# Decoder step on one core: a third PSUM bank for attention transposes, decode softmax inside the prompt attention

## Chip, cores and metric

One core of one Trainium2 chip runs the whole program. The metric is the device time of one execution in microseconds (us), the median of several runs.

## What is computed

One inference step of a hybrid decoder layer for a prompt of 1024 tokens and eight sample tokens with one query each (d = 1024, float32):

```python
qa, ka, va, logf, ub, vb, qc, kc, vc, pd = project_in(x, w_in, b_forget)
o_a = fox(qa, ka, va, cumsum(logf))        # 4 heads x 64; samples: 2048 paged rows
o_b = gelu(ub) * spatial(layer_norm(gelu(vb)))
o_c = dilated(qc, kc, vc, bias)            # 4 heads x 64; windows (128,1) (512,4) (2048,16)
o_d = pool_out(pool_mix(pd))
x = LN(ALPHA * x + (gates(x) * branches).sum() @ w_out)
x = LN(ALPHA * x + moe(x))                 # 16 SwiGLU experts, 2 per token
# fox, prompt: logits = q k^T / 8 + f_q - f_k, causal, softmax, times v
```

## The kernel before

Every engine runs its own list of instructions, written out by hand; semaphores join them, and an engine that waits holds all that is behind it. The stages are: projections in tiles of 128 tokens (`project`, L1224); the forget bias (L1301, L1303); the prompt attention of branch A (`attention(0)`); the projections `qkc` and `vpd`, between which each `decode_slot` does a step of the samples' paged attention; the prompt attention of branch C (`attention(1)`); merge, router and experts (L460 to L462 and L595).

**Forget bias.** The bias is a running sum of log forget values, needed on all partitions for 1024 keys and 4 heads. Eight groups of 4 x 128 columns are made in banks 6 and 7 in turn: per tile one matmul with a triangle (sums inside the tile) and, for all tiles but the first, one with ones (sums before the tile). VectorE copies each group to `fb` (L1771).

**Attention.** A unit is a query tile (128 rows) and a pair of heads; a pair of units, tiles 2j and 2j+1, makes one item of `values`. There are 16 units, 0 to 15, with tiles 0, 1, 0, 1, 2, 3, 2, 3 and so on to 7; units 8 to 15 have more than four key blocks and are called wide here. In `attention(br)` TensorE does, per unit u: `scores(u + 1)` (L1321, with the causal mask L1329 in branch A; banks 0 to 3), for even u `values(u // 2 - 1)` (L1349 spreads the inverse sums in bank 7, L1358 multiplies by v in bank 6, semaphore `pv`), then `transposes(u, 0)` and `transposes(u, 1)` for the two heads (L1205). Up to four key blocks of weights are transposed into bank 4, the upper ones into bank 5. VectorE adds the bias and takes the extreme (`shifted`, L1801), ScalarE exponentiates (L1580, semaphore `ex`). ScalarE copies bank 4 to SBUF (`blocks`, L1590, semaphore `pt_free0`), VectorE copies bank 5 (L1811, `pt_free1`). As there is one bank of each kind, head 1's transposes wait until head 0's are copied:

```python
pe.wait_ge(S(f"pt_free{c}"), 32 * br + n if c == 0 else 16 * br + 2 * WIDE[u] + hh)
```

`norm(i)` on VectorE (L1828, L1829) multiplies values by inverse sums and raises `on`, which the next `values` wants. In branch C `values` also carries steps of the samples (`side`): products of window values in the upper halves of banks 7 and 6 (L1420), copied by `norm` (L1824), and at item 6 `heads_out` (L1428), copied by `decode_out` (L1778).

**Samples.** POOL gathers the paged keys and multiplies them by the queries (L1967), VectorE sums (`key_sums`, L1729). The softmax over pages (`decode_softmax`: L1878 to L1892) goes back and forth between VectorE, TensorE (`top`, `spread`, `total`) and ScalarE (L1610); it begins behind the first attention. SyncE issues the weight loads, and the bias table of branch C once the scores of branch A are read.

## Time and profile before

| | |
|---|---|
| median of three runs | 1555.1 us (1554.17 to 1555.33) |
| profiled execution | 1549.21 us, span 1547.4 |
| TensorE busy in the span | 1410.2 us, 91% |
| VectorE, ScalarE, GpSimd busy | 48%, 28%, 20% |
| mean granted TensorE clock | 0.955 |

The granted clock is that of TensorE as a share of full speed (2.4 GHz). A duration of an instruction reaches to its end; matmuls overlap, so their pace is the distance between starts. "Idle before" is the time in which an engine had nothing to do ahead of an instruction, with what ended it.

### The profile page before, as it was taken

How to read it: one execution, taken by the hardware profiler on the slowest of the kernel's cores; microseconds unless marked ns; L12 is line 12 of the kernel's file. 1: busy time of each engine (PE TensorE's matmuls, PEld its weight loads, DVE VectorE, ACT ScalarE, POOL GpSimd, SP SyncE). 2: the span in 40 equal slices, each digit the busy share in tenths (PEclk: the TensorE clock that was granted, in tenths of full speed). 3: DMA queues.
4: the chain of work that ended last, by engine and by line, in shares of the span. 5: the costliest groups of instructions: out<-in, count | busy, mean ns of one | idle time of the engine just before them, and what ended most of it. 6: DMA issues, size and time to landing. Idle time of an engine off the chain costs nothing.

```text
span 1547.4 us, 20002 instructions
## 1 busy us (share of the span) xinstructions
PE 1410.2 (91%) x7544; PEld 1064.3 (69%) x7544; DVE 743.7 (48%) x1302; ACT 435.6 (28%) x723; POOL 306.5 (20%) x233
## 2 busy tenths in 40 slices
PE   7989988799998899999999999999937999999980
PEld 3466465444454589999999999968835667766650
DVE  1276454322024552243343334464675667777746
ACT  1111124301106311111111111121223555566536
POOL 1138920045165000000000000000136112221220
PEclk9979999999989999999999999999957999999995
DMA  7346630155431113222231252232277999888645
GB/s 222 100 140 224 202 135 1 52 164 186 144 123 42 35 52 99 78 91 75 78 106 64 75 189 78 63 141 76 79 299 275 371 316 324 293 296 270 195 166 223
DMA packets 75197, 237.70 MB, mean 154 GB/s; under 512 B 17030, under 2 KB 27477, under 8 KB 61423
## 3 DMA queue, kind: packets, MB, share of 16 engines
q1 hardware_dynamic: 48630, 160.73, 28.7%
q0 software_dynamic: 17792, 59.20, 13.0%
q10 hardware_dynamic: 8704, 16.84, 3.2%
q8 instruction: 43, 0.70, 0.2%
q14 instruction: 28, 0.22, 0.0%
HBM read 213.49 MB, written 65.74 MB: 180 GB/s over the span
## 4 chain that ended last, share of the span: by engine, by line
PE 79%; DVE 6%; DMA 6%; ACT 4%; POOL 3%; issue 2%; SPq 0%; POOLq 0%; DVEq 0%; ACTq 0%
PE ps L460 15%; PE ps L462 15%; PE ps L461 15%; PE ps L1224 11%; PE ps L595 6%; PE ps L1205 5%; PE ps L1321 2%; PE ps L1358 2%; DMA b<-in_w 2%; POOL b L1967 2%; DMA b<-in_cache_k,b 2%; PE ps L1409 1%; PE ps L524 1%; ACT b L1590 1%; PE ps L1239 1%
## 5 line engine op out<-in xcount | busy, mean ns | idle before, releaser
L460 PE MATMUL ps<-b,b 128*128 128x344 f32 (+1 forms) x1360 | 469.1, 345 | 5.2 <-DVE b L816 2.7
L461 PE MATMUL ps<-b,b 128*128 128x344 f32 (+1 forms) x1360 | 465.1, 342 | 0.0
L462 PE MATMUL ps<-b,b 128*128 128x344 f32 (+1 forms) x1360 | 464.9, 342 | 0.0
L460 PEld LDWEIGHTS ps<-b,b 128*128 128x128 f32 x1360 | 254.9, 187 | 24.9 <-issue 4.2
L462 PEld LDWEIGHTS ps<-b,b 128*128 128x128 f32 x1360 | 254.9, 187 | 19.0
L461 PEld LDWEIGHTS ps<-b,b 128*128 128x128 f32 x1360 | 254.7, 187 | 16.8
L1224 PE MATMUL ps<-b,b 128*128 128x512 f32 (+1 forms) x640 | 257.9, 561 | 0.0
L1224 PEld LDWEIGHTS ps<-b,b 128*128 128x128 f32 x640 | 122.3, 194 | 121.5 <-issue 116.9
L991 DVE TENSOR_TENSOR b<-b,b 128x2048 fp32r<-128x2048 f32 x64 | 146.4, 2290 | 64.1 <-ACT b L681 63.9
L1205 PE MATMUL ps<-b,b 128*128 128x128 f32 (+1 forms) x782 | 122.2, 285 | 55.0 <-DMA b<-tmp_xs 21.9
L1205 PEld LDWEIGHTS ps<-b,b 128*128 128x128 f32 (+1 forms) x782 | 93.0, 146 | 105.0 <-issue 48.8
L1059 POOL DMA_INDIRECT tmp_xs<-b,b x36 | 42.3, 1175 | 600.0 <-issue 573.9
L624 ACT ACTIVATE b<-ps,b 128x344 f32<-128x344 f32 x96 | 52.6, 548 | 379.4 <-PE ps L462 379.4
L681 ACT CAST b<-b 128x2048 fp32r<-128x2048 f32 x64 | 122.2, 1913 | 27.2 <-DMA b<-in_w 23.6
L779 DVE TENSOR_TENSOR b<-b,ps 128x344 f32<-128x344 f32 x72 | 36.9, 513 | 181.8 <-PE ps L462 181.8
L595 PE MATMUL ps<-b,b 128*128 128x512 f32 x256 | 115.3, 593 | 0.5 <-ACT b L703 0.5
L1076 POOL DMA_INDIRECT tmp_yd<-b,b x32 | 66.3, 2073 | 248.9 <-DMA tmp_yd<-b,b 219.3
L1967 POOL TENSOR_TENSOR b<-b,b 128x2048 f32<-128x2048 f32 (+1 forms) x24 | 87.7, 3656 | 35.8 <-DMA b<-in_state_k 23.3
L595 PEld LDWEIGHTS ps<-b,b 128*128 128x128 f32 x256 | 46.2, 190 | 46.7 <-issue 45.9
L1801 DVE CUSTOM_DVE_ANT_0 b<-ps,b 128x128 f32<-128x128 f32 (+7 forms) x64 | 45.9, 755 | 49.0 <-PE ps L1329 24.8
L1580 ACT ACTIVATE b<-b,b 128x128 f32<-128x128 f32 (+7 forms) x64 | 49.8, 778 | 20.9 <-DVE b L1801 20.9
L1590 ACT COPY b<-ps 128x512 f32<-128x512 f32 (+3 forms) x64 | 32.1, 502 | 74.9 <-PE ps L1205 74.7
(265 smaller groups left out, 1257.0 us busy)
## 6 DMA issues: line engine op xcount, KB each, us to landing
b<-in_w SPq DMA_DIRECT2D x96, 1024.0 KB
b<-in_w_merge SPq DMA_DIRECT2D x32, 640.5 KB, 4.3
tmp_xs<-b ACTq DMA_DIRECT2D x32, 514.0 KB, 3.8
b<-tmp_xs SPq DMA_DIRECT2D x32, 514.0 KB
b<-in_w_in SPq DMA_DIRECT2D x8, 1024.0 KB, 8.6
b<-in_xT SPq DMA_DIRECT2D x4, 1024.0 KB, 12.4
b<-in_w_out SPq DMA_DIRECT2D x4, 1024.0 KB, 7.9
b<-in_x SPq DMA_DIRECT2D x8, 512.0 KB, 4.1
```

Source lines behind the costliest of these rows:

```text
L460: mm(out, hi, mhi, start=start, stop=False)
L461: mm(out, hi, mlo, start=False, stop=False)
L462: return mm(out, lo, mhi, start=False, stop=stop)
L595: m = mm(ps[:, 2 + c, :], hT[:, u, f, :], w2[q % 3][:, f, c * 512:(c + 1) * 512], start=(f == 0), stop=(f == 1))
L624: act.activation(sg[:, j % 2, :], ps[:, (j % 2) * 2, 0:CH], ACT.Sigmoid, bias=bias).then_inc(S("sgd"), 1)
L681: act.copy(w13_hi[m % 3][:].rearrange("p k n -> p (k n)"), w13_raw[m % 4][:].rearrange("p k n -> p (k n)")).then_inc(S("w13h"), 1)
L991: dve.tensor_tensor(lo, raw, hi.bitcast(F32), ALU.subtract).then_inc(S("w13l"), 1)
L1076: pool.indirect_dma_start(a["yd"], bass.IndirectOffsetOnAxis(rt["to"][:, q % 8:q % 8 + 1], 0), yo[:, u, :], None, bounds_check=TOK - 1, oo ...
L1205: return nc.tensor.transpose(out, in_, ident[0:n, 0:n])
L1224: m = mm(ps[:, j % 2, 0:cw], xT[:, k, t * P:(t + 1) * P], w_ring[:, n % 2, k, 0:cw], start=(k == 0), stop=(k == KD - 1))
L1580: act.activation(p_, p_, ACT.Exp, scale=-1.0, bias=am[:, n % 8:n % 8 + 1], accum_out=asum[:, n % 8:n % 8 + 1]).then_inc(S("ex"), 1)
L1967: pool.tensor_tensor(out, k, q, ALU.mult).then_inc(S("kq"), 1)
```

## The change

1. The forget bias: the 28 matmuls of sums before a tile become one of 32 columns in bank 3, copied to `dsum`; VectorE adds its columns while it copies a group.
2. Head 0's lower blocks are transposed into bank 4, head 1's into bank 7, upper blocks of both into bank 5. `values` keeps its inverse sums in the upper half of bank 6. ScalarE does both exponentials of unit u + 1 ahead of the copies of an even unit u, and it also takes the upper copies of odd units.
3. The softmax of the paged decode moves into `attention(0)`: matmuls in bank 5 in `values` of items 4, 5 and 7 (`STEPS_A`), VectorE's steps behind units 0, 5, 6, 7 and 14 and in `norm`, the exponential on ScalarE behind unit 13.
4. In branch C the samples' values go to bank 5, `heads_out` from item 6 to 7, `decode_out` behind the last `norm`. Where bank 5 holds such values, the upper transposes wait for `on`.

```diff
-        SLOTS_A = {i: ["top", "spread", "total"][i:i + 1] if i < 3 else [i - 3] for i in range(18)}
+        SLOTS_A = {i: [i - 3] if i >= 3 else [] for i in range(18)}
...
-        HEADS_C = 6
+        HEADS_C = 7
+        STEPS_A = {4: "top", 5: "spread", 7: "total"}
...
+                    pe.wait_ge(S("on"), 8)
...
                 for half in range(2):
                     if n >= 2:
                         pe.wait_ge(S("fb"), n - 1)
-                    elif n == 0:
-                        pe.wait_ge(S("ob"), 5)
                     for q in range(4):
-                        t = half * 4 + q
-                        o_ = ps[:, 6 + n % 2, q * P:(q + 1) * P]
-                        mm(o_, lf[:, t, h:h + 1].to_broadcast([P, P]), tri_neg[:], start=True, stop=(t == 0))
-                        if t:
-                            m = mm(o_, lpre[:, t, h:h + 1].to_broadcast([P, P]), ones_neg[:], start=False, stop=True)
+                        m = mm(ps[:, 6 + n % 2, q * P:(q + 1) * P], lf[:, half * 4 + q, h:h + 1].to_broadcast([P, P]), tri_neg[:],
+                               start=True, stop=True)
                     m.then_inc(S("fb_mm"), 1)
                     n += 1
+                    if n == 2:
+                        mm(ps[:, 3, 0:32], ones_neg[:], lpre[:].rearrange("p t h -> p (t h)"), start=True, stop=True).then_inc(S("fb_mm"), 1)
...
-                        pe.wait_ge(S(f"pt_free{c}"), 32 * br + n if c == 0 else 16 * br + 2 * WIDE[u] + hh)
+                        if c == 1:
+                            pe.wait_ge(S("pt_free1"), 16 * br + 2 * WIDE[u] + hh)
+                            if hh == 0 and u // 2 - 1 in ((STEPS_A, VALUES_C)[br]):
+                                pe.wait_ge(S("on"), 8 * br + u // 2)
+                        elif n:
+                            pe.wait_ge(S("pt_free0"), 32 * br + n - 1)
+                        bank = 5 if c else (4, 7)[hh]
                         for k in range(4 * c, min(qt + 1, 4 * c + 4)):
-                            m = tr(ps[:, 4 + c, (k % 4) * P:(k % 4 + 1) * P], pbuf[br][n % 4][:, k * P:(k + 1) * P])
+                            m = tr(ps[:, bank, (k % 4) * P:(k % 4 + 1) * P], pbuf[br][n % 4][:, k * P:(k + 1) * P])
...
-                            mm(ps[64 * hh:64 * hh + 64, 7, a_ * P:(a_ + 1) * P], arec[:, col:col + 1].to_broadcast([P, 64]), ident[:],
+                            mm(ps[64 * hh:64 * hh + 64, 6, W + a_ * P:W + (a_ + 1) * P], arec[:, col:col + 1].to_broadcast([P, 64]), ident[:],
...
+                pe.wait_ge(S("ltot"), 1)
+                mm(ps[:, 5, 0:32], trisA[:], ltot[:], start=True, stop=True).then_inc(S("lsuf"), 1)
...
+            def side_a(i):
+                step = STEPS_A.get(i)
+                if step == "top":
+                    pe.wait_ge(S("pt_free1"), 2 * WIDE[2 * i + 2])
+                    pe.wait_ge(S("dmx"), 1)
+                    tr(ps[:, 5, 0:P], mx[:]).then_inc(S("dmx_tr"), 1)
+                elif step == "spread":
+                    pe.wait_ge(S("pt_free1"), 2 * WIDE[2 * i + 2])
+                    pe.wait_ge(S("dmc"), 1)
+                    mm(ps[:, 5, 0:32], mcol[0:32, 0:1].to_broadcast([32, P]), ident[0:32, 0:32],
+                       start=True, stop=True).then_inc(S("dmb"), 1)
+                elif step == "total":
+                    pe.wait_ge(S("pt_free1"), 2 * WIDE[2 * i + 2])
+                    pe.wait_ge(S("dsum"), 1)
+                    mm(ps[:, 5, 0:32], ones[:], dsum[:], start=True, stop=True).then_inc(S("dtot"), 1)
+
+            attention(0, bias_a, lambda k, h: va[:, k, h * 64:h * 64 + 64], side_a, tail_a)
...
-                    m = mm(ps[32 * r:32 * r + 32, bank, W:2 * W], pC[:, w:w + 32], values_c(b)[:, r, :], start=True, stop=True)
+                    m = mm(ps[32 * r:32 * r + 32, 5, half * W:(half + 1) * W], pC[:, w:w + 32], values_c(b)[:, r, :], start=True, stop=True)
...
-                for n, b in enumerate(VALUES_C.get(i, ())):
-                    values_of_c(b, 7 - n)
+                if i in VALUES_C:
+                    pe.wait_ge(S("pt_free1"), 16 + 2 * WIDE[2 * i + 2])
+                for half, b in enumerate(VALUES_C.get(i, ())):
+                    values_of_c(b, half)
                 if i == HEADS_C:
-                    heads_out(1, 7)
+                    pe.wait_ge(S("pt_free1"), 32)
+                    heads_out(1, 5)
...
-                             ps[:, 4, 0:nb * P].rearrange("p (k r) -> p k r", r=P)).then_inc(S("pt_free0"), 1)
+                             ps[:, (4, 7)[hh], 0:nb * P].rearrange("p (k r) -> p k r", r=P)).then_inc(S("pt_free0"), 1)
+
+                def high_blocks(u, hh):
+                    qt, hp = UNITS[u]
+                    if qt >= 4:
+                        act.wait_ge(S("pt1"), 16 * br + 2 * WIDE[u] + hh + 1)
+                        act.copy(pT_of(br, hh)[:, 4:qt + 1, P:2 * P],
+                                 ps[:, 5, 0:(qt - 3) * P].rearrange("p (k r) -> p k r", r=P)).then_inc(S("pt_free1"), 1)
 
                 weights(0, 0)
                 weights(0, 1)
-                for u in range(16):
+                for u in range(0, 16, 2):
+                    weights(u + 1, 0)
+                    weights(u + 1, 1)
+                    blocks(u, 0)
+                    blocks(u, 1)
                     for hh in range(2):
-                        blocks(u, hh)
-                        if u < 15:
-                            weights(u + 1, hh)
+                        blocks(u + 1, hh)
+                        high_blocks(u + 1, hh)
+                    if br == 0 and u == 12:
+                        act.wait_ge(S("dsh"), 1)
+                        act.activation(sA[:], sA[:], ACT.Exp).then_inc(S("dex"), 1)
+                    if u < 14:
+                        weights(u + 2, 0)
+                        weights(u + 2, 1)
...
+            dve.wait_ge(S("fb_mm"), 3)
+            link(dve.tensor_copy(dsum[:], ps[:, 3, 0:32]))
             for n in range(8):
-                dve.wait_ge(S("fb_mm"), n + 1)
-                dve.tensor_copy(fb[:, n // 2, (n % 2) * 512:(n % 2) * 512 + 512], ps[:, 6 + n % 2, :]).then_inc(S("fb"), 1)
+                if n >= 2:
+                    dve.wait_ge(S("fb_mm"), n + 2)
+                first = dsum[:].rearrange("p (t h) -> p h t", h=H)[:, n // 2, 4 * (n % 2):4 * (n % 2) + 4]
+                dve.tensor_tensor(fb[:, n // 2, (n % 2) * 512:(n % 2) * 512 + 512].rearrange("p (t r) -> p t r", r=P),
+                                  ps[:, 6 + n % 2, :].rearrange("p (t r) -> p t r", r=P),
+                                  first.rearrange("p (t o) -> p t o", o=1).to_broadcast([P, 4, P]), ALU.add).then_inc(S("fb"), 1)
...
-                        if u % 2 == 0:
-                            dve.wait_ge(S("pv"), 8 * br + u // 2)
-                        dve.tensor_copy(pT_of(br, hh)[:, 4:qt + 1, u % 2 * P:u % 2 * P + P],
+                        dve.wait_ge(S("pv"), 8 * br + u // 2)
+                        dve.tensor_copy(pT_of(br, hh)[:, 4:qt + 1, 0:P],
...
-                    if br:
-                        for n, b in enumerate(VALUES_C.get(i, ())):
-                            dve.tensor_copy(vo[:, b, :], ps[:, 7 - n, W:2 * W]).then_inc(S("vo"), 1)
-                        if i == HEADS_C:
-                            decode_out(1, 7)
+                    if br == 0:
+                        softmax_step(STEPS_A.get(i))
+                    else:
+                        for half, b in enumerate(VALUES_C.get(i, ())):
+                            dve.tensor_copy(vo[:, b, :], ps[:, 5, half * W:(half + 1) * W]).then_inc(S("vo"), 1)
                     to = oT[:, 2 * br, hp, j * 2 * P:(j + 1) * 2 * P]
-                    link(dve.tensor_copy(to, ps[:, 7, 0:2 * P]))
-                    dve.tensor_tensor(to, ps[:, 6, 0:2 * P], to, ALU.mult).then_inc(S("on"), 1)
+                    link(dve.tensor_copy(to, ps[:, 6, W:2 * W]))
+                    dve.tensor_tensor(to, ps[:, 6, 0:W], to, ALU.mult).then_inc(S("on"), 1)
...
-                    blocks(u, 0)
-                    blocks(u, 1)
+                    if u % 2 == 0:
+                        blocks(u, 0)
+                        blocks(u, 1)
...
+            def softmax_step(step):
+                if step == "top":
+                    dve.wait_ge(S("dmx_tr"), 1)
+                    dve.tensor_reduce(mcol[0:32, :], ps[0:32, 5, 0:P], AX.X, ALU.max).then_inc(S("dmc"), 1)
+                elif step == "spread":
+                    dve.wait_ge(S("dmb"), 1)
+                    link(dve.tensor_copy(mrow[:], ps[:, 5, 0:32]))
+                    dve.tensor_tensor(sA[:], sA[:], mA, ALU.subtract).then_inc(S("dsh"), 1)
+                elif step == "total":
+                    dve.wait_ge(S("dtot"), 1)
+                    link(dve.reciprocal(drec[:], ps[:, 5, 0:32]))
+                    dve.tensor_tensor(sA[:], sA[:], rA, ALU.mult).then_inc(S("dp"), 1)
+
+            def side_a(u):
+                if u == 0:
+                    dve.wait_ge(S("lsuf"), 1)
+                    link(dve.tensor_copy(drec[:], ps[:, 5, 0:32]))
+                elif u == 5:
+                    dve.wait_ge(S("lgb"), 16)
+                    link(dve.tensor_tensor(ltot[:], drec[:], lgb[:], ALU.add))
+                    link(dve.tensor_tensor(lfs[:, 0], lfs[:, 0],
+                                           ltot[:].rearrange("p (b o h) -> p b o h", b=NB, o=1).to_broadcast([P, NB, 16, H]), ALU.add))
+                elif u == 1:
                     key_sums(15)
+                elif u == 6:
+                    dve.wait_ge(S("ks"), 16)
+                    link(dve.scalar_tensor_tensor(s16, s16, SCALE, lfs[:, 0], ALU.mult, ALU.add))
+                elif u == 7:
+                    dve.wait_ge(S("selfd0"), N("selfd0", 16))
+                    link(dve.tensor_scalar(sA[:, :, 16, :], sA[:, :, 16, :], SCALE, None, ALU.mult))
+                    dve.tensor_reduce(mx[:, 0:32].rearrange("p (b h) -> p b h", b=NB), sA[:].rearrange("p b r h -> p b h r"),
+                                      AX.X, ALU.max).then_inc(S("dmx"), 1)
+                elif u == 14:
+                    dve.wait_ge(S("dex"), 1)
+                    dve.tensor_reduce(dsum[:].rearrange("p (b h) -> p b h", b=NB), sA[:].rearrange("p b r h -> p b h r"),
+                                      AX.X, ALU.add).then_inc(S("dsum"), 1)
...
-            last_norm = attention(1, lambda h, qt: tb[:, h, SEQ - P - P * qt:SEQ], lambda u: None)
+            last_item = attention(1, lambda h, qt: tb[:, h, SEQ - P - P * qt:SEQ], lambda u: None)
+            def last_norm():
+                last_item()
+                decode_out(1, 5)
+
```

TensorE at the start of the forget bias (`lf`, `lpre` are the sources of the sums, `fb` the semaphore of copied groups), before:

```order
L1301 MATMUL ps<-b_97984_108,b_210544_74 128x128 [waits ob,lpre,lf]
L1301 MATMUL ps<-b_97984_108,b_210544_74 128x128
L1303 MATMUL ps<-b_98496_109,b_210688_75 128x128
L1301 MATMUL ps<-b_97984_108,b_210544_74 128x128
L1303 MATMUL ps<-b_98496_109,b_210688_75 128x128
L1301 MATMUL ps<-b_97984_108,b_210544_74 128x128
```

and now, from the first group to the first scores:

```order
L1300 MATMUL ps<-b_97984_108,b_210544_74 128x128 [waits ob,lpre,lf]
L1300 MATMUL ps<-b_97984_108,b_210544_74 128x128 x7
L1305 MATMUL ps<-b_210688_75,b_98496_109 128x32
L1300 MATMUL ps<-b_97984_108,b_210544_74 128x128 [waits fb]
...
L1300 MATMUL ps<-b_97984_108,b_210544_74 128x128 [waits fb]
L1300 MATMUL ps<-b_97984_108,b_210544_74 128x128 x3
L1385 MATMUL ps<-b_96832_105,b_96960_106 128x32 [waits qkT_qka,ltot,evicted,fb]
L1321 MATMUL ps<-b_148480_55,b_140288_54 128x128 x2
```

Of the pairs of L1301 and L1303 only the triangles are left (L1300), with one matmul for all sums (L1305); L1385, for the decode's sums, stood behind the attention.

ScalarE around units 10 and 11 of `attention(0)`, before (`b_132096` and `b_164864` take the transposed weights of head 0 and 1):

```order
L1590 COPY b_132096_119<-ps 128x4x128 [waits pv,pt0]
L1580 ACTIVATE b_49536_115,b_211104_82<-b_49536_115,b_211072_81 128x768 [waits sc_free]
L1590 COPY b_164864_120<-ps 128x4x128 [waits pv,pt0]
L1580 ACTIVATE b_53632_116,b_211104_82<-b_53632_116,b_211072_81 128x768 [waits sc_free]
L1590 COPY b_132096_119<-ps 128x4x128 [waits pt0]
L1580 ACTIVATE b_201232_113,b_211104_82<-b_201232_113,b_211072_81 128x896 [waits sc_free]
L1590 COPY b_164864_120<-ps 128x4x128 [waits pt0]
L1580 ACTIVATE b_205328_114,b_211104_82<-b_205328_114,b_211072_81 128x896 [waits sc_free]
```

and now:

```order
L1603 ACTIVATE b_49536_115,b_211104_82<-b_49536_115,b_211072_81 128x768 [waits sc_free]
L1603 ACTIVATE b_53632_116,b_211104_82<-b_53632_116,b_211072_81 128x768 [waits sc_free]
L1613 COPY b_132096_119<-ps 128x4x128 [waits pv,pt0]
L1613 COPY b_164864_120<-ps 128x4x128 [waits pv,pt0]
L1613 COPY b_132096_119<-ps 128x4x128 [waits pt0]
L1620 COPY b_132096_119<-ps 128x2x128 [waits pt1]
L1613 COPY b_164864_120<-ps 128x4x128 [waits pt0]
L1620 COPY b_164864_120<-ps 128x2x128 [waits pt1]
L1603 ACTIVATE b_201232_113,b_211104_82<-b_201232_113,b_211072_81 128x896 [waits sc_free]
L1603 ACTIVATE b_205328_114,b_211104_82<-b_205328_114,b_211072_81 128x896 [waits sc_free]
```

Both exponentials of unit 11 have moved ahead of the copies of unit 10; the two copies of `128x2x128` are the upper blocks of unit 11, from VectorE.

VectorE at unit 12 of `attention(0)` (`b_92672` holds the paged scores), before:

```order
L1828 COPY b_33024_50<-ps 128x256 [waits pv]
L1829 TENSOR_TENSOR b_33024_50<-ps,b_33024_50 128x256 [waits dve_chain]
L1811 COPY b_132096_119<-ps 128x3x128 [waits pv,pt1]
L1811 COPY b_164864_120<-ps 128x3x128 [waits pv,pt1]
L1801 ISA b_201232_113,b_211072_81<-ps,b_173056_58 128x896 [waits pt1,sc]
```

and now:

```order
L1843 ISA b_53632_116,b_211072_81<-ps,b_173056_58 128x1024 [waits pt1,sc]
L1843 ISA b_211072_81 128x1
L1902 COPY b_96448_102<-ps 128x32 [waits dmb,pv]
L1903 TENSOR_TENSOR b_92672_91<-b_92672_91,b_96448_102 128x544 [waits dve_chain]
L1869 COPY b_33024_50<-ps 128x256
L1870 TENSOR_TENSOR b_33024_50<-ps,b_33024_50 128x256 [waits dve_chain]
L1852 COPY b_132096_119<-ps 128x3x128 [waits pv,pt1]
L1852 COPY b_164864_120<-ps 128x3x128 [waits pv,pt1]
```

The copy and subtraction L1902 and L1903 stand between the shifts and `norm`, thus ahead of `on`.

## Rows read from the trace of the kernel before

**Rows 1.** Stretch A:B, length; busy PE, PEld, DVE, ACT, POOL (x instructions); clock; DMA; GB/s

```profile
192.40:211.90 19.50, 15.55 (x125) 15.16 (x122) 10.70 (x13) 0.82 (x1) 10.87 (x5) 0.91 0.77 274
...
199.20:203.40 4.20, 4.20 (x23) 4.20 (x24) 1.18 (x2) 0.00 (x0) 3.09 (x3) 0.59 0.68 260
...
211.90:302.10 90.20, 78.89 (x608) 50.10 (x608) 39.33 (x103) 41.50 (x101) 0.00 (x0) 1.00 0.03 10
302.10:309.23 7.13, 1.42 (x6) 0.98 (x6) 5.12 (x12) 0.00 (x0) 3.23 (x6) 0.75 0.53 149
466.10:549.83 83.73, 71.52 (x560) 43.27 (x561) 42.38 (x116) 40.00 (x96) 19.48 (x23) 0.98 0.11 36
```

**Rows 2.** TensorE in order of time, forget bias (L1301, L1303): start, duration, idle before

```profile
199.15 0.71 PE L1301 MATMUL ps<-b,b 128*128 128x128 f32 x4 [3.17 <-DVE b L1771]
...
206.24 0.39 PE L1301 MATMUL ps<-b,b 128*128 128x128 f32 x2
```

**Rows 3.** Waits in the two attentions: us in total, times, longest

```profile
DVE b L1801 <- PE ps L1329: 24.8, 15, 2.5
...
PE ps L1205 <- ACT b L1590: 9.7, 17, 0.8
...
PE ps L1205 <- ACT b L1590: 8.9, 16, 0.8
```

**Rows 4.** TensorE in order of time: transposes of units 5 and 13

```profile
229.92 0.60 PE L1205 MATMUL ps<-b,b 128*128 128x128 f32 x4
231.29 0.63 PE L1205 MATMUL ps<-b,b 128*128 128x128 f32 x4 [0.77 <-ACT b L1590]
...
273.89 1.04 PE L1205 MATMUL ps<-b,b 128*128 128x128 f32 x8
275.25 0.63 PE L1205 MATMUL ps<-b,b 128*128 128x128 f32 x4 [0.33 <-ACT b L1590]
...
277.22 1.99 PE L1321 MATMUL ps<-b,b 64*128 64x512 f32 x8
```

**Rows 5.** Groups of instructions (busy, mean ns of one | idle before), and one piece of VectorE's time

```profile
L1729 DVE TENSOR_REDUCE b<-b 128x32 f32<-128x2048 f32 x16 | 36.4, 2284 | 21.3 <-POOL b L1967 20.8
...
L1829 DVE TENSOR_TENSOR b<-ps,b 128x256 f32<-128x256 f32 x16 | 6.8, 424 | 0.6
...
L1801 DVE CUSTOM_DVE_ANT_0 b<-ps,b 128x896 f32<-128x896 f32 x8 | 8.4, 1088 | 5.9 <-PE ps L1329 3.4 <-PE ps L1321 2.5
...
L1590 ACT COPY b<-ps 128x512 f32<-128x512 f32 x40 | 23.2, 581 | 56.1 <-PE ps L1205 56.1
...
L1771 DVE COPY b<-ps 128x512 f32<-128x512 f32 x8 | 5.4, 688 | 8.0 <-PE ps L1303 8.0
...
L1801 DVE CUSTOM_DVE_ANT_0 b<-ps,b 128x128 f32<-128x128 f32 (+7 forms) x64 | 45.9, 755 | 49.0 <-PE ps L1329 24.8
L1580 ACT ACTIVATE b<-b,b 128x128 f32<-128x128 f32 (+7 forms) x64 | 49.8, 778 | 20.9 <-DVE b L1801 20.9
...
507.63 0.76 DVE L1824 COPY b<-ps 128x256 f32<-128x256 f32 x2 [2.29 <-PE ps L1358]
```

**Rows 6.** TensorE, then VectorE, in order of time behind the first attention

```profile
307.82 0.48 PE L1205 MATMUL ps<-b,b 128*128 128x128 f32 x1 [4.29 <-DVE b L1878]
...
309.23 8.73 PE L1224 MATMUL ps<-b,b 128*128 128x512 f32 x16
...
318.38 7.11 PE L1224 MATMUL ps<-b,b 128*128 128x512 f32 x16
...
306.66 1.10 DVE L1878 TENSOR_REDUCE b<-b 128x32 f32<-128x544 f32 x1
...
309.56 0.72 DVE L1884 TENSOR_TENSOR b<-b,b 128x544 f32<-128x544 f32 x1
```

**Rows 7.** End of the second attention: VectorE's `decode_out`, TensorE's weight loads of the merge

```profile
539.54 0.70 DVE L1778 COPY b<-ps 64x8 f32<-64x8 f32 x4 [6.93 <-PE ps L1358]
...
554.37 0.19 PEld L460 LDWEIGHTS ps<-b,b 128*128 128x128 f32 x1 [0.78 <-DVE b L794]
```

31 lines of the change are left out of this document (7 added, 24 removed).

## The prediction

> **What bounds the kernel now.** I read first the busy time by stretch [rows 1]. TensorE is busy for 78.9 of the 90.2 us of the first attention and 71.5 of the 83.7 us of the second, VectorE and ScalarE for about half or less: TensorE's own order sets the pace, and only its gaps can be won. Around the first attention stand two worse stretches: before it 19.5 us with TensorE busy for 15.6, and behind it 7.1 us (302.1 to 309.2) with 1.4 busy. Then come the waits [rows 3]: in each attention the transposes wait 16 or 17 times for the copy L1590 of ScalarE, 9.7 and 8.9 us together. The last step is the order of time on TensorE at the places which the change touches [rows 2, 4, 6].
>
> **1. Forget bias.** Now there are 32 + 28 matmuls. At full clock a record follows the one before by 0.11 us (two in 0.39, of which the last one's own length is 0.28), and each matmul has two records: 0.22 [rows 2]. Two groups of four are made, then TensorE waits 3.17 us until VectorE (late with sums of keys) starts to copy, and six groups follow from 199.15. The granted clock over 199.2 to 203.4 is 0.59 [rows 1], so mostly the lower of the two levels (1.2 GHz), behind that gap. In the change one matmul replaces 28, and the addition goes into the copy (L1771, 0.69 a group). I leave its price as it is, because `norm`'s product L1829 reads 256 columns of a bank and a buffer in 0.42 where the plain copies L1824 take 0.38 each [rows 5]; 0.04 more a group stays under TensorE's 0.9. A copy of 32 columns is put ahead, so the six groups start at 199.4. With the clock low until 203.4 as now, about ten of their 24 matmuls are done by then, and 14 x 0.22 = 3.1 remain: 206.4, the last addition 207.2, the small matmul for the decode sums, first scores at 207.5 where they start at 211.9 now. **-4.4 us.** Bounds: the gap is now 4.9 us long, and a low clock for another 2 us costs 1 (-3.4); no low clock at all gives -5.8.
>
> **2. Transposes, narrow units** (query tiles 0 to 3; units 0 to 7). The transposes of head 1 start 1.37 us behind those of head 0 for four blocks (229.92, 231.29) [rows 4]; a block takes 0.11 (eight in 1.04, less the last one's length), so 0.93 is lost. In total, the waits and 0.17 for each modelled end: 9.7 + 17 x 0.17 = 12.6, and 8.9 + 16 x 0.17 = 11.6. With head 1 in bank 7 its transposes follow at once. The eight narrow units lose 0.6 to 0.9 each, some 6.3 together. Not all comes back. In unit 0 and 1 ScalarE now does both exponentials of unit 1 ahead of the first copies, and the sum of keys on VectorE (2.3 us) holds the reciprocal: 0.7 stays. Behind unit 7 the scores of the next tile need both banks of each head, thus both of VectorE's shifts of the unit before (1.09 each for tile 6 [rows 5], so some 0.8 for tile 4), while the transposes of unit 7 now take only 0.9: 0.7 late. **-4.9, and -5.0 in the second attention.**
>
> **3. Wide units** (tiles 4 to 7; units 8 to 15). Bank 5 is still single, so head 1's upper blocks wait for head 0's upper copy. An odd unit with tile 7 takes 3.33 us now (273.89 to 277.22) [rows 4]. Then: lower blocks to 0.44, upper to 0.88; ScalarE's lower copy from 0.64 to 1.12 and its upper one to 1.6 (0.58 busy [rows 5], 0.1 of it overlapped); head 1's upper blocks 1.66 to 2.1. That saves 1.2; tile 5 by the same sum 0.7 to 1.3. In an even unit VectorE's norm must be over first (two of 0.42), then its upper copy: 1.5 to 1.9 us instead of 2.1 to 3.0. The even units 10 and 12 of each attention get a new wait: their upper blocks wait for `on`, as bank 5 holds decode values. Queued behind it are head 1's transposes and the next scores. In the first attention `norm` does a small maximum more in unit 10 (gain nil) and in unit 12 a copy and the subtraction of 0.72 [rows 6]: `on` 2.0 us behind `pv`, the unit 1.1 us slower than now. In the second it does two copies (0.76) first, 0.5 us slower each. Further, the scores of units 11 to 13 wait about 0.4 once for VectorE's shifts, which were hidden behind longer transposes. Unit by unit, 8 to 15: 0.6 + 0.7 + 0 + 0.8 - 1.1 + 1.2 + 1.1 + 0.3 = **-3.6**; in the second attention 0.6 + 0.8 - 0.5 + 0.8 - 0.6 + 1.4 + 2.0 (units 14 and 15 together) = **-4.5**.
> Bounds on 2 and 3 together: nothing if each wait comes back elsewhere, 28 if none does (24 and the few waits for L1811). Around my 18 I keep 5 to 24.
>
> **4. Softmax of the paged decode.** Behind the first attention TensorE stands while VectorE norms, adds and takes a maximum (4.29 idle before 307.82) [rows 6], and goes on at 309.23: the first projection of 16 records takes 8.73 us, the one at 318.38 takes 7.11. The change puts these steps into the units: adds and maximum on VectorE at units 5 to 7, the exponential on ScalarE behind unit 13, the sum at unit 14. What hides them: VectorE idles 24.8 us in 15 pieces before its shifts [rows 3], and the longest new step (maximum 1.10) at unit 7 ends just before `values` wants the reciprocal; ScalarE's exponential lies behind 6 us of scores and values. If that cover is gone, the steps' length comes back, about 4 us. Gone: 7.1 of the gap and 1.6 of the slow projection, **-8.7**. Added in the attention: three small matmuls of about 0.3, **+0.9**. `on` = 8 is now wanted by the transposes behind the next projection, 7 us later, so it is hidden. The gathers on POOL and SP's weights are issued behind the same semaphores as now and keep their distances.
>
> **5. End of the second attention.** The 32 tiny matmuls move from `values(6)` to `values(7)` at the same cost, and `decode_out` goes behind the last norm: 0.84 us (0.70 and its link) [rows 7] ahead of VectorE's split, for which TensorE waits 0.78 already. All of it is late: **+0.8**.
>
> **Sum:** -4.4 - 4.9 - 3.6 - 5.0 - 4.5 - 8.7 + 0.9 + 0.8 = **-29.4 us**. The profiled execution takes 1549.2 (span 1547.4) and would take 1519.8; the median of the three runs, 1555.1, is 5.9 above it, and 1555.1 - 29.4 gives **1526 us**. What comes after (merge, experts) starts earlier and is as before. About 0.2%, 3 us, is what a measurement can tell from no change.
>
> **Rivals.**
> A, *the attention becomes a chain of latencies* (22%). Without waits for bank 4 TensorE runs into exponentials and shifts that are some tenths late in every unit. For it: two such places came up above, both in narrow units. Against it: both helpers are half idle. Then the attentions give 5 in place of 18: 1526 + 13 = 1539.
> B, *ScalarE's new order* (3%), the slow side. The copies of an even unit now stand behind both exponentials of the next unit. If the scores of that unit end only as the transposes start, each copy comes one shift (mean 0.76) and two exponentials (mean 0.78) [rows 5] later, 2.3 us; over 16 even units 37: 1526 + 37 = 1563. It decides where the scores end less than 2.3 us ahead of the transposes. `values` lies between, above 3 us in the last pairs but about 1 in the first, whose exponentials are short; so it can bite only there.
> C, *the clock* (1%). The granted clock is 1.00 over the first attention and 0.98 over the second, with 33 gaps of up to 0.8 us in them [rows 1, 3]: such gaps do not lower it here. Should three banks in turn lower it for a quarter of the 150 us of busy time, 37 are lost as well: 1563. The Trainium skill, "TensorE: Matmul & The Clock Gate", section "A second HAM failure mode: psum-queue depth-cycling", tells of a kernel in which cycling through banks left small idles that made the clock swing, and so speaks against this change; by that rule the time would be C's. No run here shows it for gaps of this size.
> D, *the softmax in the units does not hide* (8%): 4 us on VectorE, and 3 more at `on`: 1526 + 7 = 1533.
> My forecast has the remaining 66%.
>
> **Range.** Low: -5.8 in 1, -24 in 2 and 3 and the rest as forecast give -37, or 1518; all at once is unlikely, and I take 1519. High: 1539, A. B and C, 4%, lie outside, with the lower half of A's outcomes. Faster by over 0.2%: 0.94; within 0.2%: 0.02; slower: 0.04.
>
> **What would show it.** First scores 4 to 5 us earlier; the transposes' waits for copies under 5 us in an attention instead of 9; the first attention at about 83 us, the second at 74; no gap behind the first attention, and the first projection there at 7.1 us; a wait of 1 to 1.5 us before the upper transposes of units 10 and 12; TensorE's wait for the split at 1.6 instead of 0.8. The prediction is wrong if as many waits for exponentials replace those for copies, if scores wait for shifts in all wide units, or if the clock falls inside an attention.

## The result and the profile after

The changed kernel takes 1535.83 us (median of 4 runs, 1534.79 to 1536.08) against 1554.63 for the kernel before on the same chip (1552.33 to 1555.33). The ratio is 0.9887, with a 95% interval of 0.9872 to 0.9902. The medians lie 18.8 us apart (1.1% by the ratio): faster as forecast and inside the range, but less than two thirds of the 29.4 us. The profiled execution takes 1534.79 (span 1533.0, granted clock 0.952), 14.4 us less span than before: the profiled execution of before (1549.21) was 5.4 us below its median, that of after 1.0 below, so the stages below account for 14.4 us and not for all of the gain.

The windows of after that answer to [rows 1] (length; busy PE, PEld, DVE, ACT, POOL, each with its count of instructions; clock; DMA; GB/s), the last two being new:

```profile
191.00:199.40 8.40, 2.11 (x20) 2.00 (x18) 5.33 (x6) 0.77 (x1) 5.79 (x3) 0.93 0.89 289
199.40:203.40 4.00, 3.14 (x14) 3.14 (x15) 2.06 (x4) 0.00 (x0) 2.12 (x1) 0.50 0.54 213
...
209.40:294.30 84.90, 79.03 (x614) 50.94 (x613) 40.13 (x105) 45.69 (x110) 0.08 (x1) 1.00 0.09 33
294.30:301.30 7.00, 7.00 (x19) 3.11 (x18) 2.98 (x8) 0.00 (x0) 3.23 (x6) 1.00 0.38 121
...
354.00:370.70 16.70, 13.08 (x100) 6.23 (x99) 2.30 (x4) 1.37 (x5) 8.83 (x12) 0.80 0.57 191
...
520.90:533.00 12.10, 12.01 (x66) 9.09 (x64) 0.00 (x0) 0.09 (x1) 0.00 (x0) 0.58 0.01 1
```

The first attention is 84.9 us instead of 90.2 and TensorE never stands behind it. Two stretches are new trouble: TensorE is busy for 13.1 of 16.7 us from 354.0, and its clock is 0.58 over the last 12 us of the second attention.

Waits of TensorE in the first attention, then in the second (total, times, longest), to be set beside [rows 3]:

```profile
PE ps L1206 <- DVE b L1870: 2.0, 2, 1.4
PE ps L1206 <- ACT b L1620: 1.1, 4, 0.3
...
PE ps L1321 <- DVE b L1843: 0.8, 2, 0.7
...
PE ps L1206 <- DVE b L1852: 0.6, 3, 0.2
PE ps L1206 <- ACT b L1613: 0.4, 1, 0.4
...
PE ps L1206 <- DVE b L1870: 2.3, 2, 1.1
PE ps L1206 <- ACT b L1620: 1.1, 4, 0.3
```

The 9.7 and 8.9 us for ScalarE's copies have become 0.4 + 1.1 and 0.5 + 1.1; the largest wait that is left is the new one for `on` (L1870). The length of a projection behind the attention answers to [rows 6]: 7.13 where it was 8.73.

Now the two places where time was lost. TensorE in order of time (start, duration, idle before): the forget bias, `values_a(6)` with the projection behind it, and the heads of the second attention.

```profile
191.02 1.95 PE L1300 MATMUL ps<-b,b 128*128 128x128 f32 x16
192.81 0.31 PE L1305 MATMUL ps<-b,b 128*128 128x32 f32 x2
200.26 8.04 PE L1300 MATMUL ps<-b,b 128*128 128x128 f32 x48 [7.15 <-DVE b L1811]
...
360.00 1.93 PE L1433 MATMUL ps<-b,b 128*32 128x256 f32 x16 [3.62 <-issue]
361.87 8.91 PE L1225 MATMUL ps<-b,b 128*128 128x512 f32 x16
...
521.04 5.70 PE L1452 MATMUL ps<-b,b 128*128 128x2 f32 x32
```

Then the products of keys on GpSimd and VectorE's sum and additions at the forget bias, and GpSimd's gathers of values, in order of time:

```profile
192.55 4.51 POOL L2037 TENSOR_TENSOR b<-b,b 128x2048 f32<-128x2048 f32 x1
197.10 2.29 DVE L1765 TENSOR_REDUCE b<-b 128x32 f32<-128x2048 f32 x1 [2.81 <-POOL b L2037]
...
199.52 1.29 DVE L1811 TENSOR_TENSOR b<-ps,b 128x512 f32<-128x512 f32 x2
...
201.28 4.62 POOL L2037 TENSOR_TENSOR b<-b,b 128x2048 f32<-128x2048 f32 x1 [4.22 <-DMA b<-in_cache_k,b]
...
316.52 1.03 POOL L2001 DMA_INDIRECT b<-in_cache_v,b  x1 [0.17 <-issue]
317.55 1.64 POOL L2020 DMA_DIRECT2D b<-in_state_k  x3
...
323.72 1.80 POOL L2037 TENSOR_TENSOR b<-b,b 128x768 f32<-128x768 f32 x1 [4.00 <-DMA b<-in_state_k]
325.69 1.00 POOL L2001 DMA_INDIRECT b<-in_cache_v,b  x1 [0.16 <-issue]
...
353.85 1.03 POOL L2001 DMA_INDIRECT b<-in_cache_v,b  x1 [0.16 <-issue]
```

The additions start behind VectorE's sum of keys 14 (197.10), and that behind the product of keys 14 (192.55 to 197.07). The product with a wait of 4.22 us (201.28) is that of keys 15; it ends at 205.9, long behind the first addition, and its sum is made in the attention (213.81).

A wait "for issue" on TensorE names no releaser, but `values_a(6)` waits for nothing late other than the sixth gather, `load_values(6)`. That gather is issued at 353.85 and TensorE wants it at 356.4 (360.00 - 3.62). A step of GpSimd's chain (gather, window keys, 4 us of waiting for them, product) takes 9.2 us here (325.69 - 316.52); TensorE's slot takes 8.5 to 8.9 and is the faster of the two. In the kernel before, the same gather was issued 10 us ahead of its use:

```profile
362.94 1.03 POOL L1931 DMA_INDIRECT b<-in_cache_v,b  x1 [0.16 <-issue]
...
372.94 1.05 PE L1409 MATMUL ps<-b,b 128*32 128x256 f32 x16
```

Because many experiments follow, I cut each trace at the same places of TensorE's order. The lengths in us: A, first forget-bias matmul to first scores; B, from there to the first 128x512 projection matmul behind the attention's last scores; C, to `values_a(0)`; D, to the last `values_a`; E, to the first scores of the second attention; F, to the first matmul of the merge. "Start" is the moment of the first cut. It differs by up to 6.5 us between executions although no edit lies ahead of it, the part behind the last cut by up to 3.5 us (997.6 to 1001.1), and E and F by some us with the clock. The runs were taken in rounds on different chips, each with the kernel before beside it (medians 1552.8 to 1554.6), so "won" is counted from the before of the same round; between rounds this is the fairer number.

| kernel | start | A | B | C | D | E | F | median us | won |
|---|---|---|---|---|---|---|---|---|---|
| before | 192.5 | 19.4 | 79.2 | 34.8 | 113.8 | 26.4 | 83.7 | 1554.6 | - |
| after | 191.0 | 18.4 | 73.5 | 26.2 | 120.3 | 24.6 | 79.0 | 1535.8 | 18.8 |
| e1_bias_alone | 190.9 | 17.4 | 79.2 | 35.6 | 113.9 | 27.2 | 83.8 | 1553.4 | 1.1 |
| e2_softmax_back | 192.6 | 15.5 | 69.9 | 36.2 | 117.8 | 26.4 | 77.3 | 1536.0 | 18.6 |
| e3_values_first | 192.5 | 15.4 | 73.5 | 26.2 | 113.9 | 28.7 | 77.3 | 1527.9 | 26.7 |
| e4_sums_behind | 193.9 | 12.9 | 74.3 | 26.2 | 119.6 | 30.4 | 79.0 | 1534.5 | 20.0 |
| e5_old_order | 189.6 | 18.9 | 76.4 | 26.2 | 120.5 | 27.5 | 79.5 | 1535.3 | 18.5 |
| e6_one_bank | 192.6 | 17.7 | 80.1 | 26.2 | 121.3 | 27.5 | 89.6 | 1547.3 | 6.4 |
| e9_before_values_first | 191.9 | 19.9 | 79.2 | 34.6 | 113.9 | 27.5 | 88.1 | 1553.3 | 0.4 |
| e10_back_values_first | 192.4 | 15.6 | 69.9 | 36.5 | 113.9 | 27.4 | 77.3 | 1533.8 | 19.9 |
| e8_both | 192.9 | 11.3 | 74.3 | 26.2 | 113.8 | 26.6 | 77.3 | 1525.1 | 27.7 |
| e11_reader | 194.2 | 16.2 | 72.5 | 26.2 | 113.8 | 26.4 | 74.4 | 1525.2 | 27.6 |
| e12_all_three | 189.7 | 12.1 | 73.3 | 26.2 | 113.8 | 27.0 | 76.0 | 1519.4 | 33.4 |
| e13_bias_undone | 187.7 | 15.5 | 73.3 | 26.2 | 113.9 | 26.1 | 74.4 | 1523.6 | 29.7 |

### The profile page after: what moved, and what is told of

Its sections match the earlier page's. It is cut to its first block, busy times and chain, and to the rows that moved or that the text cites. A ratio compares the mean times of both kernels' runs of the same rounds, so it can differ in the third digit from the quotient of the medians.

```text
span 1533.0 us, 19911 instructions
## 1 busy us (share of the span) xinstructions
PE 1404.3 (92%) x7490; PEld 1059.1 (69%) x7490; DVE 730.0 (48%) x1288; ACT 442.2 (29%) x739; POOL 302.7 (20%) x233
## 4 chain that ended last, share of the span: by engine, by line
PE 79%; DMA 6%; DVE 5%; POOL 4%; ACT 3%; issue 2%; SPq 0%; POOLq 0%; DVEq 0%; ACTq 0%
PE ps L461 15%; PE ps L463 15%; PE ps L462 15%; PE ps L1225 11%; PE ps L596 6%; PE ps L1206 5%; POOL b L2037 3%; PE ps L1364 2%; PE ps L1321 2%; DMA b<-in_w 2%; DMA b<-in_cache_k,b 1%; PE ps L1433 1%; PE ps L525 1%; PE ps L1240 1%; DMA tmp_yd<-b,b 1%
## 5 line engine op out<-in xcount | busy, mean ns | idle before, releaser
L463 PEld LDWEIGHTS ps<-b,b 128*128 128x128 f32 x1360 | 254.9, 187 | 19.4 <-issue 0.8
L1206 PE MATMUL ps<-b,b 128*128 128x128 f32 (+1 forms) x782 | 118.8, 285 | 37.2 <-DMA b<-tmp_xs 21.5
L682 ACT CAST b<-b 128x2048 fp32r<-128x2048 f32 x64 | 122.3, 1913 | 26.4 <-DMA b<-in_w 22.7
L1077 POOL DMA_INDIRECT tmp_yd<-b,b x32 | 63.2, 1974 | 252.7 <-DMA tmp_yd<-b,b 223.2
L2037 POOL TENSOR_TENSOR b<-b,b 128x2048 f32<-128x2048 f32 (+1 forms) x24 | 87.5, 3648 | 40.8 <-DMA b<-in_state_k 23.3
L1765 DVE TENSOR_REDUCE b<-b 128x32 f32<-128x2048 f32 x16 | 36.5, 2284 | 34.3 <-POOL b L2037 34.1
```

What stands on the lines that cost most here:

```text
L463: return mm(out, lo, mhi, start=False, stop=stop)
L682: act.copy(w13_hi[m % 3][:].rearrange("p k n -> p (k n)"), w13_raw[m % 4][:].rearrange("p k n -> p (k n)")).then_inc(S("w13h"), 1)
L1077: pool.indirect_dma_start(a["yd"], bass.IndirectOffsetOnAxis(rt["to"][:, q % 8:q % 8 + 1], 0), yo[:, u, :], None, bounds_check=TOK - 1, oo ...
L1206: return nc.tensor.transpose(out, in_, ident[0:n, 0:n])
L2037: pool.tensor_tensor(out, k, q, ALU.mult).then_inc(S("kq"), 1)
```

## The experiments

**e1, the forget-bias edit alone on the kernel before** (part 1 of the change, nothing else).

> The kernel before with the forget-bias edit alone (one matmul for the sums of whole tiles, added by VectorE in its copy). In the full change the stage became 1.0 us shorter where 4.4 were forecast: TensorE stood 7.15 us instead of 3.17 before the first addition, because VectorE's sum of keys waited for GpSimd's product, and that 4.22 us for a gather of keys. Theory M (a matter of the moment at which the gather runs): the edit does not touch the gathers, so with the wait at about 3.2 us the first scores start 3.4 to 4.4 us earlier than in before, and the time is 3 to 4.5 us shorter. Rival S (structural: the shorter work of TensorE always meets VectorE's late sums of keys): the wait is near 5 to 7 us and only 0.5 to 1.5 us are won. In both the attentions are as in before.

Measured: 1553.42 us, ratio 0.999 (0.9974 to 1.0007), so no gain that can be told from none. A is 2.0 us shorter. TensorE waited 5.96 us for the first addition: it came to this stage 1.5 us earlier than in before (190.9 instead of 192.5) and was through its two groups sooner, but the additions could start only at the same time (TensorE goes on at 198.98, in before at 199.15). That is rival S, whose numbers fit as well (5 to 7 us of wait, 0.5 to 1.5 us won). The gather of keys on which the expectation puts the 7.15 us belongs to keys 15, and nothing at the forget bias waits for those.

**e2, the softmax back behind the attention** on the changed kernel.

```diff
-        STEPS_A = {4: "top", 5: "spread", 7: "total"}
+        STEPS_A = {}
-            qk_evict("qkc", 1, 1)
+            decode_softmax(0, sA, lambda: qk_evict("qkc", 1, 1), lambda: None)
```

> The full change with only the paged softmax put back behind the first attention (adds, maximum, exponential, sum, product and the three small matmuls as before). Theory G (given back): in the changed kernel the gap behind the attention went (8.8 us), but the stage of the next projections became 6.3 us longer, because GpSimd's chain of window keys and value gathers, 9.1 to 9.6 us a step against TensorE's 8.5 to 8.9, had its slack in that gap; so putting the softmax back costs only about 2.5 us (between 1 and 4), the gap of about 8.8 us returns and the wait of 3.6 us before values_a(6) is gone. Rival N (the 6.3 us have another cause, for example the new order of the gathers or a disturbed run): putting it back costs 8 us or more and the stage keeps its 130 us.

Measured: 1535.98, ratio 0.9868 (0.9837 to 0.99), nothing lost on the median. C shows the gap back, 36.2 for 26.2:

```profile
295.06 0.47 PE L1206 MATMUL ps<-b,b 128*128 128x128 f32 x1 [4.64 <-DVE b L1939]
```

B is 3.6 us shorter without the softmax in the units. So the move takes 10.0 out and puts 3.6 in, and the rest of its worth went elsewhere. D is 117.8 and not 113.8, as GpSimd once waited 7.14 us for window keys and `values_a(8)` then 2.08 for its gather: even with the gap the slack can be used up.

**e3, each gather of values one step earlier** on GpSimd, nothing else changed.

```diff
+            pool.wait_ge(S("dv"), 1)
+            load_values(2)
             key_step_c(0)
             key_step_c(1)
-            for s in range(2, 16):
-                pool.wait_ge(S("dv"), s - 1)
-                load_values(s)
-                if s < NB:
-                    pool.wait_ge(S("ks"), 16 + s - 1)
-                    keys_c(s)
-                    key_step_c(s)
+            for s in range(3, 17):
+                if s <= NB:
+                    pool.wait_ge(S("ks"), 16 + s - 2)
+                    keys_c(s - 1)
+                if s < 16:
+                    pool.wait_ge(S("dv"), s - 1)
+                    load_values(s)
+                if s <= NB:
+                    key_step_c(s - 1)
```

> The full change with one edit on GpSimd: each gather of values is issued one step earlier, ahead of the product of window keys of the step before (load_values(2) before key_step_c(0), load_values(s) before key_step_c(s-1)). Theory G: the wait of 3.6 us before values_a(6) at 360 us and the low clock behind it (0.9 + 1.8 us) come from the gather of values that was issued too late; with the edit both go, and the kernel takes 5.5 to 6.5 us less than the changed one (near 1529.5). Rival N (the wait is for something else, or the window keys then come late for VectorE): less than 2 us won, the wait stays or turns up before the transposes.

Measured: 1527.9, ratio 0.9823 (0.9795 to 0.9851), 7.9 us less than the changed kernel; D fell by 6.5. GpSimd in order of time now waits for TensorE, not the other way round, and TensorE goes from the tiny matmuls straight into `values_a(6)`:

```profile
343.85 1.03 POOL L2001 DMA_INDIRECT b<-in_cache_v,b  x1 [3.02 <-PE ps L1433]
```

```profile
352.97 1.94 PE L1222 MATMUL ps<-b,b 128*8 128x128 f32 x64
354.72 1.05 PE L1433 MATMUL ps<-b,b 128*32 128x256 f32 x16
355.70 4.56 PE L1225 MATMUL ps<-b,b 128*128 128x512 f32 x10
```

**e4, the sum of keys 14 behind the additions** of the forget bias.

```diff
-                key_sums(6 + i)
+                if i < 8:
+                    key_sums(6 + i)
...
+            key_sums(14)
+            dve.wait_ge(S("ks"), 15)
```

> The full change with VectorE's sum of keys 14 moved from ahead of the forget-bias additions to behind them. Theory: the 7.15 us wait before the first addition shrinks to about 2 (additions start once the queries of the last tile are out, 194.3), the clock behind it stays higher, the sum costs up to 1.3 us before the first shift: 3 to 5 us less than the changed kernel. Rival (the stage is bound by GpSimd's chain anyhow, since sums 14 and 15 are only moved): under 1 us won, with a wait of 2 us or more in the first units of the attention.

Measured: 1534.54, ratio 0.986 (0.983 to 0.989). A is 5.5 us shorter (wait 2.18 instead of 7.15), B 0.8 longer, E 5.8 longer: there TensorE waited 3.17 us (after: 1.50) for a copy that VectorE makes behind the write of `out_pool`, a transfer, and the clock was low for 13.7 us of E instead of 3.4. On the median only 1.3 us is left, which the scatter (1528.5 to 1539.2) covers. Inconclusive by itself.

**e5, ScalarE's old order in even units.**

```diff
-                    weights(u + 1, 0)
-                    weights(u + 1, 1)
                     blocks(u, 0)
+                    weights(u + 1, 0)
                     blocks(u, 1)
+                    weights(u + 1, 1)
```

> The full change with one edit: in even units ScalarE copies a head's lower blocks before it takes the next unit's exponential of that head, as before the change (copy, exponential, copy, exponential, where the change has two exponentials, then two copies). Theory (the order is worth little once each head has a bank of its own): both attentions stay within 1 us of the changed kernel, first scores to last scores 60.5 and 55.7 us, and the time within 2 us. Rival B (the new order delays each copy by a shift and two exponentials): this kernel is then 5 us or more faster than the changed one. Rival B' (the new order is what makes three banks work): this kernel is 4 us or more slower.

Measured: 1535.26, ratio 0.9884 (0.9859 to 0.9909), the same as the changed kernel. B is 2.9 longer in a profiled execution that was the slowest of four (clock 0.97 over the first 62.5 us, where after has 1.00), and first to last scores of the second attention 57.0 instead of 55.7. Of the 2.9 us, 1.7 are the low clock (3.4 us of it at half speed), so the new order is worth about 1 us an attention in the traces; the medians do not show it (1535.3 against 1535.8). Rival B, by which this kernel had to be 5 us faster, is out, and so is B'.

**e6, also the lower transposes of both heads in bank 4 again.**

```diff
-                        elif n:
-                            pe.wait_ge(S("pt_free0"), 32 * br + n - 1)
-                        bank = 5 if c else (4, 7)[hh]
+                        else:
+                            pe.wait_ge(S("pt_free0"), 32 * br + n)
+                        bank = 5 if c else 4
```

> The full change with the old order of ScalarE as in the run before and, in addition, the lower transposes of both heads in bank 4 again (each group waits for the copy of the one before). Theory (parts 2 and 3: the second bank takes the waits for copies away): first scores to last scores grow from 60.5 to about 65.5 us in the first attention and from 55.7 to about 61.5 in the second, and the kernel takes 8 to 12 us more than the run with old order and two banks. Rival A (the attention is a chain of latencies, banks hardly matter): under 4 us more, with the waits for exponentials and shifts smaller by what the waits for copies grow.

Measured: 1547.3, ratio 0.996 (0.9946 to 0.9975), 12.0 us more than e5. The waits for copies are back (these are those of the first attention; the second has 8.6 as well):

```profile
PE ps L1206 <- ACT b L1613: 8.6, 15, 0.8
```

The other waits of that attention shrank from 4.3 us in e5 to 0.9, so some of what A describes is there, but rival A's "under 4 us" is out. (F of 89.6 overstates it: the clock was 0.67 over the first 20.6 us of that attention.)

**e9, the early gathers on the kernel before.** The edit of e3.

> The kernel before with the edit on GpSimd alone (each gather of values issued one step earlier). The runs so far: with this edit the changed kernel came to 1527.9 us from 1535.8, and the changed kernel with the softmax put back took 1536.0, with a wait of 2.1 us before a values_a too. Theory G (only the changed kernel lacks slack): no more than 1 us won on 1554.6, and the stage from values_a(0) to the last values_a stays at 113.8 us. Rival V (in before too, some executions wait for the gathers, which is why the median of its runs lies above the profiled one): 2 to 5 us won on the median, and less scatter between its runs.

Measured: 1553.29, ratio 0.9995 (0.9982 to 1.0009): no gain, D 113.9. Theory G holds and rival V falls.

**e10, softmax back and early gathers.** The edits of e2 and e3.

> The full change with the softmax put back behind the attention and the gathers of values issued one step earlier. With the late gathers the move of the softmax was worth nothing (1536.0 with it put back, 1535.8 in the changed kernel). By the traces the move takes 10.0 us out between the first projection and values_a(0) (36.2 to 26.2) and puts 3.6 us into the first attention (69.9 to 73.5 from first scores to the first projection). Theory G (the late gathers hid the gain): here the gap is back and nothing waits for gathers, so this kernel takes 5 to 7 us more than the 1527.9 of the changed kernel with the early gathers, near 1534. Rival (the move gains nothing whatever the gathers do): 1526 to 1530.

Measured: 1533.81, ratio 0.987 (0.9844 to 0.9896). With late gathers the move of the softmax was worth 0.2 us (1536.0 against 1535.8), with early ones 5.9 (1533.8 against 1527.9; 6.8 by what each won over the before of its round), where the traces promise 10.3 - 3.6 = 6.7. A wait of TensorE ahead of a `values_a`, of 2.1 to 4.5 us, stands in the profiled executions of all five kernels that have the changed attention and late gathers (after, e2, e4, e5, e6), and in none of the seven with early ones.

**e8, early gathers and the sum behind the additions.** The edits of e3 and e4.

> The changed kernel with the early gathers of values and, in addition, the sum of keys 14 behind the forget-bias additions (each alone: 1527.9 and 1534.5). By the traces the moved sum makes the stretch from the first forget-bias matmul to the first scores 12.9 us instead of 15.4, while the first attention takes 0.8 us more and the bands 1.8. Theory (additive, the price of the bands is a matter of one execution): 1 to 3 us less than 1527.9. Rival (what is won ahead of the attention is lost behind it, where VectorE waits for a transfer): within 1 us of 1527.9.

Measured: 1525.06, ratio 0.982 (0.9803 to 0.9837), 2.8 us less than e3. Over the before of its own round it won 27.7 and e3 26.7, so the medians do not tell the theory (1 to 3 us) from the rival (within 1). The traces speak for the theory: A and B together take 85.6 us where e3 has 88.9, and E is 26.6, so the long E of e4 was a matter of that execution.

**e11, early gathers, and the upper transposes freed by the last read of bank 5.**

```diff
-                                pe.wait_ge(S("on"), 8 * br + u // 2)
+                                if br:
+                                    pe.wait_ge(S("vo"), N("vo", NB + 1 + VALUES_C[u // 2 - 1][1]))
+                                else:
+                                    pe.wait_ge(S("five"), {4: 1, 5: 2, 7: 3}[u // 2 - 1])
```

> The changed kernel with the early gathers of values, and the upper transposes of the units that share bank 5 with decode values wait for the last read of that bank (a semaphore behind the maximum, the copy or the reciprocal, or that of the two decode copies) instead of for the norm's product behind it. Theory (the waits of 2.0 and 2.3 us in the attentions are the norm's two operations, 0.8 us each time, and the rest is the reads themselves): the waits shrink to about 0.8 and 0.9 us, and 1.5 to 3 us are won, near 1525.5. Rival (VectorE's upper copy stands behind the norm anyway and the wait only moves to head 1's transposes): under 1 us won, the wait for L1852's copies grows by as much.

Measured: 1525.17, ratio 0.9829 (0.9815 to 0.9842), 2.7 us less than e3 on the median, but 0.9 by what each won in its round. In the traces B is 1.0 shorter and F 2.9, of which 1.3 lie ahead of the last scores and 1.6 behind them, where the clock was low for 3.4 us instead of 6.8. Waits of the first attention, then of the second:

```profile
PE ps L1206 <- DVE b L1855: 1.8, 4, 1.0
```

```profile
PE ps L1206 <- DVE b L1870: 0.7, 2, 0.4
```

In the first attention 1.2 us of the wait moved to the upper copy (0.6 before), as the rival said; in the second it really went (2.3 to 0.7).

**e12, all three edits.**

> The changed kernel with all three edits: early gathers, sum 14 behind the additions, upper transposes released by the last read of bank 5. If the three are additive, by the traces: 2.5 - 0.8 us from the sum and 1.5 to 3 us from the release, 1523 to 1526. If the release only moves a wait, 1526 to 1528.

Measured: 1519.37 (1516.25 to 1522.45), ratio 0.9784 (0.9766 to 0.9802). It is below what was expected and the fastest of all: 33 us under the kernel before, 16 under the changed one. It is 5.7 us under e8 and 5.8 under e11, of the same round, where the traces show 2.3 (B and first to last scores) and 3.3 (A and B) for the edit that was added. In the profiled executions 3.2 of the 4.3 us that e12 has less than e8 lie ahead of the first cut, where the code is the same. So the excess over the sum is not explained by the edits.

**e13, the forget bias as before** in the kernel of e12: 60 matmuls, plain copies.

> The fastest kernel so far (all three edits, 1519.4) with the forget bias as before: 60 matmuls in eight groups, plain copies. There VectorE's sum of keys no longer stands ahead of the copies, so this prices the forget-bias edit without that delay. Theory (the matmuls left out are on the path as soon as VectorE is not late): 21 of the 27 matmuls left out belong to the six groups behind the first copies, at 0.22 us each at full clock 4.6 us, so first forget-bias matmul to first scores grows from 12.1 to 16.5 to 17.5, and the time by 4 to 5.5 us, to about 1524. Rival (the edit is worth 1 us or so whatever VectorE does, as its worth of 1.0 in the changed kernel and 1.1 alone suggest): under 2 us more.

Measured: 1523.6, ratio 0.9809 (0.9795 to 0.9823), 4.2 us more on the median (3.8 by what each won in its round), though the two intervals overlap a little. A grows from 12.1 to 15.5, 3.4 us. The edit is worth its matmuls once VectorE is not late.

## Why the prediction was right, and where it was too high

**Forget bias: -4.4 forecast, -1.0 in A, 2.5 us earlier first scores.** The count of matmuls and the price of an addition (0.69) were right. The step that failed was the wait, taken as "now 4.9 us long": it was 7.15 in the profiled execution and 5.96, 5.25 and 4.66 in e1, e2 and e3. Its end follows GpSimd and not TensorE. In the ten kernels with the sum of keys 14 ahead of the additions (or copies) TensorE goes on 3.0 to 3.2 us behind the end of GpSimd's product of keys 14, and that end lies between 195.8 and 198.5 us. Its beginning moves with TensorE, from 189.6 to 194.2 for the first matmul of the stage. Against the forecast, after lost 1.4 us in A because TensorE came earlier (191.0 instead of 192.5, which A shows as a loss and the time does not), 0.9 because the product ended later (197.07 instead of 196.18), and about 1.1 behind it, where the clock stayed low until 205.0 and not 203.4. A of e2 and e3, 3.9 and 4.0 less than before, is what the edit gives when the two meet as they did in before. The bound of -3.4 was too tight, as it left out that the thing waited for is itself a chain with a scatter.

**Narrow units: right.** The transposes of unit 8 come 28.8 us behind the first scores in after where it was 33.4: -4.6, forecast -4.9; second attention 30.0 to 25.1, forecast -5.0.

**Wide units: right in the first attention.** e10, which has the new banks and no softmax, has B 9.3 shorter; less 4.6, the wide units gave 4.7, which is the forecast of 3.6 with the 1.1 for unit 12's `on` taken back. In the second, first to last scores (the first matmul of each) fell by 6.4 (62.1 to 55.7), forecast 7.5. Behind them the last two units should give 2.0 and gave nothing in e2, e3, e8 and e10 (21.6 us to the merge, as in before). Why they did not I have not found out; F as a whole fell by 4.8 in after and 6.4 in these four, where 9.5 was forecast.

**Softmax: the gap right, its price and the gathers behind it wrong.** Gone are 8.6 us of C, forecast 8.7. In the units it costs 3.6 (e2 and e10 against e3), where I had 0.9 and 1.1: both units 10 and 12 wait for `on`, not one. The large error is the sentence that the gathers on GpSimd "keep their distances". They kept their semaphores, but not their distance: GpSimd's chain starts from the end of the attention and moved by 7.7 us (302.39 to 294.70 for its first window keys), TensorE's `values_a(0)` by 16.7 (325.86 to 309.12). The slack of the sixth gather fell from 10 us to 2.5, under the 6 that it takes to land. D grew by 6.5: 3.6 of waiting, and most of the rest at a low clock behind it.

**End of the second attention: +0.8 forecast, right.** TensorE's weight load waits 1.62 to 1.63 us in all executions with the new order and 0.78 or 0.79 in the three with the old one. Not counted was that the clock is low behind the 32 tiny matmuls. Windows of the kernel before, behind its heads, then of after, during and behind them:

```profile
534.40:542.00 7.60, 6.84 (x46) 4.27 (x46) 1.97 (x7) 1.89 (x4) 0.00 (x0) 0.78 0.42 162
```

```profile
521.00:526.70 5.70, 5.66 (x34) 5.64 (x34) 0.00 (x0) 0.00 (x0) 0.00 (x0) 0.63 0.01 3
526.70:533.00 6.30, 6.30 (x33) 3.45 (x32) 0.00 (x0) 0.00 (x0) 0.00 (x0) 0.52 0.00 0
```

Length times missing clock is 1.7 us before, and 2.1 + 3.0 after (an estimate from these rows). But this is not the move from `values(6)` to `values(7)`: the low stretch at these heads is 3.4 to 6.8 us long in the three executions with the old place and 3.4 to 10.3 us in the eleven with the new one. Last scores to merge took 21.6 us before and 23.2 after, and 21.6 (e1) to 23.3 (e9) with the code as before, 20.0 to 23.2 in the kernels with the heads in item 7. A cost of the move beyond the 0.8 is not shown.

**The sum by cuts**, of the profiled executions: -1.4 ahead of the first cut (not by the change), -1.0, -5.7, -8.6, +6.5, -1.8, -4.8, and +2.4 behind the last one (0.8 of it the split) are -14.4, as the span. The 4.4 us by which the medians differ more are not in these two profiles. The only profile of the old attention in a slower execution, e9 (1556.0), has F of 88.1 instead of 83.7, with a low clock from 469.1 to 475.9 us; that may be a part of it, but is not shown.

**How much was luck.** The mechanism was right for the banks and for the gap behind the attention. But 1535.8 lies inside the range only because its upper end was set for rival A, which did not happen; what cost the most, 6.5 us in D, had no term. Without the late gathers the forecast would nearly have held: e3 takes 1527.9, and 1526 was forecast (26.7 us won in its round, 29.4 forecast). Even this agreement is in part luck, as its span is only 20.4 us below that of before: the forecast put the same gain on the median as on a profiled execution that was a quick one.

**The rivals.** A fell with e6, B with e5. Of C the profiled execution shows nothing: granted clock 1.00 over 209.4 to 294.3 with the transposes going round three banks. The Trainium skill, "TensorE: Matmul & The Clock Gate", section "A second HAM failure mode: psum-queue depth-cycling", tells of a kernel in which the clock swings; taken as a rule it should do so here, and this trace does not agree. One of the others shows a little of it: in e5 the clock was low from 265.1 to 268.5, behind the new wait for `on` of unit 12, with TensorE busy for 1.83 of the 3.40 us before the fall. It cost 1.7 us there (an estimate, half of 3.4). After has the same wait (1.4 us) and no fall.

```profile
263.12 0.95 PE L1206 MATMUL ps<-b,b 128*128 128x128 f32 x7 [1.35 <-DVE b L1870]
```

Of D's 7 us the units show 1.6 (3.6 where 0.9 and 1.1 were counted). What cost more was in no rival: the change took away the gap in which another engine's queue caught up.
